# Weights of a two-layer decoder step stored in the order in which the kernel loads them

## The reference

```python
# mixers: dense projections in and out
proj = h @ w_in                              # mLSTM: (1024, 3088), NSA: (1024, 2608)
y = o @ w_out                                # (1024, 1024)

# NSA, compressed branch: blocks of 32 keys through a small MLP, first layer w1[c, 32, 64, 64]
first  = einsum('bnlcgd,cldh->bncgh', sub, w1[:, :16])
second = einsum('bnlcgd,cldh->bncgh', sub, w1[:, 16:])
ckv = einsum('bncgh,chd->bncgd', gelu(first[:, :-1] + second[:, 1:] + b1), w2)

# PEER, for each token
q = (x @ w_q).reshape(blk, 8, 256)           # w_q: (1024, 2048)
s1 = einsum('nhd,hkd->nhk', q[..., :128], sub_keys[:, 0])
s2 = einsum('nhd,hkd->nhk', q[..., 128:], sub_keys[:, 1])
# top 16 of each, top 16 of their 256 sums -> expert (8 heads x 16), gate = softmax
act = gelu(einsum('nd,nhkd->nhk', x, u_tab[expert]))
out = einsum('nhk,nhkd->nd', gate * act, v_tab[expert])
```

## Time and profile before

| | us |
|---|---|
| median of three runs | 2446.6 |
| the three runs | 2443.54, 2446.6, 2453.86 |
| the profiled execution | 2442.64 |
| its span, first to last instruction | 2440.4 |
| PE busy, DVE busy, POOL busy, ACT busy | 1919.6, 1482.9, 1445.5, 723.1 |
| moved by DMA | 805.62 MB, mean 330 GB/s |
| mean granted TensorE clock | 0.891 of full speed |

### The profile page before, as it was taken

The page is one execution under the profiler, slowest core; times in us unless marked ns, Lnnn a source line. Parts: engine busy times, 40 slices in busy tenths (PEclk is TensorE's granted clock), DMA queues, the critical chain, the costliest instruction groups (busy, mean ns, idle before and its releaser), DMA issues. The chain is left out here.

```text
span 2440.4 us, 22610 instructions
## 1 busy us (share of the span) xinstructions
PE 1919.6 (79%) x6982; PEld 949.8 (39%) x6982; DVE 1482.9 (61%) x3404; ACT 723.1 (30%) x1737; POOL 1445.5 (59%) x1285
## 2 busy tenths in 40 slices
PE   8997995999787776987879689875678777859666
PEld 6453682444343333545422255462123323313211
DVE  2234467885656544585884457759357776774753
ACT  2022122787556111421111125211123333312101
POOL 2111056668778775676677567744467666457674
PEclk9998997999898786898899879897899998979879
DMA  9053259999999999899999998998889999899897
GB/s 304 5 219 116 74 183 372 351 347 355 408 399 398 405 397 373 307 358 403 355 409 400 386 387 312 366 357 288 324 323 397 383 363 395 327 335 399 299 349 279
DMA packets 253950, 805.62 MB, mean 330 GB/s; under 512 B 41796, under 2 KB 46408, under 8 KB 244360
## 3 DMA queue, kind: packets, MB, share of 16 engines
q0 software_dynamic: 176496, 673.82, 72.5%
q1 hardware_dynamic: 77192, 130.37, 15.1%
q10 hardware_dynamic: 144, 0.00, 0.0%
HBM read 798.37 MB, written 14.04 MB: 333 GB/s over the span
## 5 line engine op out<-in xcount | busy, mean ns | idle before, releaser
L3259 PE MATMUL g_acc<-g_vrow,g_diag 128*128 128x512 f32 (+1 forms) x1524 | 812.0, 670 | 236.1 <-DMA g_vrow<-in_peer_v_dram,f_idx 131.3
L3113 POOL DMA_INDIRECT f_u<-in_peer_u_dram,f_idx x576 | 655.0, 1137 | 429.9 <-DVE g_dot L3200 170.3
L3129 POOL DMA_INDIRECT g_vrow<-in_peer_v_dram,f_idx x576 | 678.1, 1177 | 341.5 <-issue 145.6
L3200 DVE CUSTOM_DVE_ANT_0 f_u<-f_u,f_h 128x1024 f32<-128x1024 f32 x576 | 692.3, 1219 | 205.2 <-DMA f_u<-in_peer_u_dram,f_idx 160.2
L3259 PEld LDWEIGHTS g_acc<-g_vrow,g_diag 128*128 128x128 f32 (+1 forms) x1524 | 279.0, 197 | 686.5 <-issue 513.1
L3173 DVE SCALAR_TENSOR_TENSOR x<-g_vrow,g_w,x 128x1024 f32<-128x1024 f32 x195 | 249.7, 1281 | 93.1 <-DMA g_vrow<-in_peer_v_dram,f_idx 84.6
L3225 ACT ACTIVATE g_diag<-const,g_w 128x128 f32<-128x128 f32 (+1 forms) x381 | 132.0, 379 | 185.3 <-DVE g_w L3156 171.7
L1295 PE MATMUL g_side<-g_slab 128*128 128x512 f32 (+3 forms) x288 | 124.1, 570 | 46.5 <-DMA g_slab<-in_nsa_w_in_dram 45.9
L1155 PE MATMUL g_side<-g_slab 128*128 128x512 f32 x256 | 135.9, 614 | 4.2 <-ACT g_slab L1193 2.5
L2276 PE MATMUL g_side<-g_cmp_kT,g_q_blk 128*32 128x512 f32 x160 | 87.7, 632 | 41.6 <-DVE g_cmp_kT L2407 28.3
L1193 ACT ACTIVATE g_slab<-g_more 64x256 f32<-64x256 f32 x256 | 96.7, 378 | 63.5 <-PE g_more L1144 60.3
(11 more groups left out here) (418 smaller groups left out, 2427.2 us busy)
## 6 DMA issues: line engine op xcount, KB each, us to landing
g_slab<-in_nsa_w_in_dram SPq DMA_DIRECT2D x15, 2048.0 KB, 19.6
g_slab<-in_peer_w_q_dram SPq DMA_DIRECT2D x14, 2048.0 KB, 20.8
g_slab<-in_nsa_w_out_dram SPq DMA_DIRECT2D x6, 2048.0 KB, 21.3
f_u<-in_peer_u_dram,f_idx POOLq DMA_INDIRECT x576, 8.2
g_vrow<-in_peer_v_dram,f_idx POOLq DMA_INDIRECT x576, 8.0
g_slab<-in_state_win_kv_dram SPq DMA_DIRECT2D x8, 1024.0 KB, 8.6
out_win_s_dram<-in_state_win_kv_dram SPq DMA_DIRECT2D x1, 8128.0 KB
f_u<-in_mlstm_w_in_dram SPq DMA_DIRECT2D x2, 2048.0 KB, 17.2
```

The costliest lines, as they stand in the source:

```text
L3113: pool.indirect_dma_start(u[:, i % RU, :], None, u_table, bass.IndirectOffsetOnAxis(ap=idx[:, col:col + 1], axis=0), element_offset=layer ...
L3129: pool.indirect_dma_start(vrow[:, i % RV, :], None, v_table, bass.IndirectOffsetOnAxis(ap=idx[:, col:col + 1], axis=0), element_offset=lay ...
L3200: dve.tensor_tensor_reduce(row, row, h[:, t, :], 1.0, 0.0, ALU.mult, ALU.add, dot[:, g % 2, k:k + 1]).then_inc(dotted, 1)
L3259: mm = pe.matmul(acc[0:n, a, :], diag[:, q % (2 * GRP), 0:n], vrow[:, i % RV, a * 512:a * 512 + 512], start=first and on_pe[i] == on_pe[GR ...
```

## The change

The host lays out three kinds of weights anew before the launch; the kernel's loads follow.

- The five dense weights are stored as blocks of 512 columns, each [partition, chunk, column], so that a partition's 16 KB are one run. The columns left over (16 of the mLSTM input weight, 48 of the NSA input weight) are an array of their own, `<name>_rest`, in the same order.
- The sub-keys are stored as [d, head half, key]. SP loads them into `keys_T` itself. The transposes on PE, the copies on ACT and their semaphores go, in both routes; in the first route PE waits for `copied` 5 in their place, in the prompt's route the scores wait for `keys_in`.
- The compression's first layer is stored as [(position in pair, d), pair, half, h], and each of its two parts is one load with 4 KB per partition; the counts of the waits follow (7 loads become 5).

The same bytes are loaded, at the same points of SP's order. The core of the diff:

```diff
+def in_blocks(w):
+    layers, _, n = w.shape
+    full = n // WB * WB
+    w = w.reshape(layers, DC, P, n)
+    blocks = w[..., 0:full].reshape(layers, DC, P, n // WB, WB).transpose(0, 3, 2, 1, 4)
+    rest = w[..., full:].transpose(0, 2, 1, 3)
+    return blocks, rest
+
+def weight_block(I, name, layer, col, n):
+    if n == WB:
+        return I[name][layer, col // WB]
+    return I[name + "_rest"][layer]
...
 # front_stage, sync
-                    sp.dma_start(blocks[j][:], weight[:, :, col:col + n]).then_inc(w_in[j], 16)
+                    sp.dma_start(blocks[j][:], weight_block(I, "mlstm_w_in", 0, col, n)).then_inc(w_in[j], 16)
...
 # CachedBlocks.load_weights; the same in PromptWork.sync
         for c in range(2):
-            for f in range(2):
-                sp.dma_start(self.w1[:, c, :, f], I["nsa_cmp_w1"][0, c, f * CSTR:(f + 1) * CSTR].rearrange(
-                    "(k l) d h -> (l d) k h", l=2)).then_inc(self.weights_in, 16)
+            sp.dma_start(self.w1[:, c], I["nsa_cmp_w1"][0, c]).then_inc(self.weights_in, 16)
...
-    LOADS = 2 * 2 + 2 + 1
+    LOADS = 2 + 2 + 1
...
 # Projection.load; likewise w_out and w_q in PromptWork, RouteWork, DecodeWork, FirstRoute and the mLSTM stage
-        w_in = self.S.I["nsa_w_in"][0].rearrange("(c p) n -> p c n", p=P)
-        sp.dma_start(self.ring[t // 2][:, k % 2, :, 0:cols], w_in[:, :, col:col + cols]).then_inc(self.S.w_in[k % 2], 16)
+        sp.dma_start(self.ring[t // 2][:, k % 2, :, 0:cols], weight_block(self.S.I, "nsa_w_in", 0, col, cols)).then_inc(self.S.w_in[k % 2], 16)
...
 # PromptWork.sync, first tile
-            sp.dma_start(route.keys, I["peer_sub_keys"][1].rearrange("h s k d -> k (h s) d")).then_inc(route.keys_in, 16)
+            sp.dma_start(S.keys_T, I["peer_sub_keys"][1]).then_inc(route.keys_in, 16)
...
 # RouteWork.scores
-            pe.wait_ge(self.keys_copied, 2 * NJ)
+            pe.wait_ge(self.keys_in, 32)
...
 # FirstRoute.pe
         pe.wait_ge(self.keys_in, 16)
-        for k in range(NJ):
-            if k >= 2:
-                pe.wait_ge(self.keys_copied, k - 1)
-            self.turn_keys(pe, k)
-        pe.wait_ge(self.keys_copied, NJ)
+        pe.wait_ge(self.copied, 5)
...
 # FirstRoute.act; likewise in RouteWork.act
-        for k in range(NJ):
-            act.wait_ge(self.keys_turned, k + 1)
-            act.activation(S.keys_T[:, 4 * k:4 * k + 4, :], self.bank[k % 2].rearrange("p (c k) -> p c k", c=4), ACT.Copy
-                           ).then_inc(self.keys_copied, 1)
...
+def first_layer_of_blocks(w1):
+    layers = w1.shape[0]
+    w = w1.reshape(layers, 2, 2, CSTR // 2, 2, ADH, ADH)
+    return w.transpose(0, 1, 4, 5, 3, 2, 6).reshape(layers, 2, P, CSTR // 2, 2, ADH)
...
 # kernel(): laid_out = {**inputs, "const": CONST}
+    laid_out["peer_sub_keys"] = laid_out["peer_sub_keys"].transpose(0, 4, 1, 2, 3).reshape(-1, PK, HH, PK)
+    laid_out["nsa_cmp_w1"] = first_layer_of_blocks(laid_out["nsa_cmp_w1"])
+    for name in IN_BLOCKS:
+        laid_out[name], rest = in_blocks(laid_out[name])
```

More of the change, by code:

```diff
@@ L1859, in sync @@
         for c in range(2):
[L1860 to L1863, removed]
+            sp.dma_start(self.w1[:, c], I["nsa_cmp_w1"][0, c]).then_inc(self.cw_in, 16)
         for a in (1, 0):
@@ L1868, in sync @@
                 sp.wait_ge(self.multiplied, t + 1)
[L1869 removed]
+            sp.dma_start(proj.ring[0][:, a], weight_block(I, "nsa_w_out", 0, a * WB, WB)).then_inc(S.w_in[a], 16)
         sp.wait_ge(proj.saved, 16 * (3 * t + 3))
@@ L1999, in __init__ @@
         self.q_T = place(11264, [P, HH, P])
-        self.keys = place(15504, [P, HH, P])
         self.gain = place(13312, [P, D])
-        self.keys_in, self.keys_turned, self.keys_copied, self.q_stored, self.scored = (
-            st.sem("q_" + n) for n in ("keys_in", "keys_turned", "keys_copied", "stored", "scored"))
+        self.keys_in, self.q_stored, self.scored = (st.sem("q_" + n) for n in ("keys_in", "stored", "scored"))
     PROJ = 10
@@ L2036, in pe @@
             yield from at(p0 + b)
-            if t == 0 and b in (-2, 0, 2, 4):
-                self.turn_keys(pe, (b + 2) // 2)
             j, r = divmod(b, 6)
@@ L2082, in act @@
         p0 = beat + self.PROJ
-        if t == 0:
-            for k in range(NJ):
-                yield from at(p0 - 1 + 2 * k)
-                act.wait_ge(self.keys_turned, NJ + k + 1)
-                act.activation(S.keys_T[:, 4 * k:4 * k + 4, :], S.bank[k % 2].rearrange("p (c k) -> p c k", c=4),
-                               ACT.Copy).then_inc(self.keys_copied, 1)
         for j in range(NJ):
@@ L2691, with __init__ @@
 class FirstRoute:
-    def __init__(self, st, S, ranks, keys, u_ring, v_ring, more, acc, w_out_in, d_scores):
+    def __init__(self, st, S, ranks, keys_in, u_ring, v_ring, more, acc, w_out_in, d_scores):
         self.S, self.ranks, self.w_out_in = S, ranks, w_out_in
-        self.keys_in, self.keys_turned, self.keys_copied = keys
+        self.keys_in = keys_in
         place = S.slab.place
-        cmp_kT = S.cmp_kT[:].rearrange("p b a k -> p (b a k)")
         cmp_v = S.cmp_v[:].rearrange("p b g -> p (b g)")
@@ L2706, in __init__ @@
         self.q_TL = place(12800, [P, 4, P + NDEC])
-        self.keys = inside(cmp_kT, 0, [P, HH, P])
         self.gain = inside(cmp_v, 0, [P, D])
@@ L2739, in out @@
         mm.then_inc(self.summed, 1)
-    def turn_keys(self, pe, k):
-        for c in range(4):
-            mm = pe.transpose(self.bank[k % 2][:, c * P:(c + 1) * P], self.keys[:, 4 * k + c, :], self.S.M.ident)
-        mm.then_inc(self.keys_turned, 1)
     def project(self, pe, j):
@@ L3001, in __init__ @@
         self.route = RouteWork(st, S, self.proj, self.ranks)
-        keys = (self.route.keys_in, self.route.keys_turned, self.route.keys_copied)
-        self.first = FirstRoute(st, S, self.ranks, keys, u_ring, v_ring, more, acc, w_out_in, d_scores)
+        self.first = FirstRoute(st, S, self.ranks, self.route.keys_in, u_ring, v_ring, more, acc, w_out_in, d_scores)
         self.cached = CachedBlocks(st, S, self.first, [more[:, 0], more[:, 1]])
@@ L3356 @@
     arrays, I, O = {}, {}, {}
-    for name, value in {**inputs, "const": CONST}.items():
+    laid_out = {**inputs, "const": CONST}
+    laid_out["peer_sub_keys"] = laid_out["peer_sub_keys"].transpose(0, 4, 1, 2, 3).reshape(-1, PK, HH, PK)
+    laid_out["nsa_cmp_w1"] = first_layer_of_blocks(laid_out["nsa_cmp_w1"])
+    for name in IN_BLOCKS:
+        laid_out[name], rest = in_blocks(laid_out[name])
+        if rest.size:
+            laid_out[name + "_rest"] = rest
+    for name, value in laid_out.items():
         a = np.ascontiguousarray(value)
```

44 lines of the change are left out of this document (14 added, 30 removed).

## The result

The changed kernel takes 2385.7 us (median of four runs, 2371.9 to 2391.8) beside 2447.4 us for the kernel before: 61.7 us less, ratio 0.974 (95% interval 0.969 to 0.9785). The profiled execution of the changed kernel is the longest of its four, 2391.8 us (span 2389.6), 50.9 us less than the profiled one of before. 2386 was forecast. The total came out; several of the terms that make it up did not, and the rest of this text is about those.

The account below looks back on a forecast made before the run. No engine alone was taken as the bound: the DMA engines had 239 us of unfilled time in the interleaved stage, partly from late weight loads. Nine terms summed to 60.8 us (17 to 94), giving 2386 us, range 2353 to 2430.

Parts of the forecast that it names:

- A: First route, before the first gather: key transposes and copies removed, PE turns the normed tile sooner; gain 2.0 us (0 to 2.5).
- B: Cached blocks' start: the first layer comes some 35 us earlier, so DVE's late start goes; gain 11.3 us (2 to 21.6).
- C: First prompt tile: PE's waits for block 4 and first layer, mostly covered by DMA work; gain 4 us (1 to 5.5).
- G: Decode projection: PE short, two waits for blocks of 8.66 and 10.34 us go; gain 18 us (10 to 23).
- D: First prompt tile's route: PE's 7.45 us wait for a query block; gain 5 us (0 to 7.1).
- E: Second prompt tile: the same weight waits as in the first, as little room; gain 2 us (0 to 3.2).
- F: Second tile's route: PE's 8.46 us wait for query block 2 delays DVE's ranking; gain 8.5 us (4 to 13).
- H: Decode output: DVE's 6.53 us wait for joined parts, queued behind a 2 MB block; gain 5 us (0 to 8).
- I: Whole interleaved stage: cheaper transfers, 401 GB/s rising towards 409 during loads, over 37 blocks; gain 5 us (0 to 10).
- first rival: Dense blocks land no sooner; only keys and first layer gain, 17 us, total 2429 us; chance 0.13.
- second rival: Gather queue is the bound all along, engines freed earlier find no rows; gain 10 us, total 2437 us; chance 0.09.
- The third: Slower: 16 KB rows starve gathers during loads, 4.2 us per block where rings are empty; 2470 us at 20 blocks; chance 0.06.

Follow-up runs that it names:

- the first execution: First profiled execution of the changed kernel, no edit, against the one profiled execution of the kernel before: 2391.8 us, 50.9 us less.
- the three executions: Three profiled executions of the unedited changed kernel, each against the profiled execution of before: 50.9, 57.6 and 55.5 us gained.
- the first-layer experiment: Changed kernel with only the compression's first layer loaded as before, four loads of 256 KB with 256-byte runs: 2413.3 us, ratio 0.9847.
- the two repeats: The changed kernel measured twice more with no edit, beside other runs: 2387.7 us (ratio 0.9745) and 2381.5 us (ratio 0.9719).

## Why the prediction was right in sum, and where not

**Why the loads were late** was right in its core: time goes by rows, as many of one queue as of the other; that a turn is a single row, as the text had it, is not shown. The model's 15.4, 10.2 (for 4 KB) and 6.4 us stand beside 14.8, 9.9 to 10.0 and 6.1 to 8.0 us of rows. (The lower bound, 2.1 MB at 409 GB/s, is 5.1 us, not 5.2.) The landing of 8 us failed: 11.5. The step is "8 us with the latency by which the measured values exceed the model": it took 1.6 us from loads that stood in line behind one another, so that their time to the first row was already covered. With the queue empty most loads of the stage show about 3.5 us from SP's issue to its first row (1666.87 to 1670.31 in the kernel with a place for the gate columns) and 0.6 to 0.8 from the last row to PE. So "no wait above 3 us" failed as well: 6.88 us for block 4 in the first tile and 6.51 for the gate columns are left.

**The packets** fell by 53,600, not 59,000. Counted by size, blocks went from 46,080 rows to 5,760, the first layer from 12,288 to 768; but the gate columns stayed at 3,072 rows of 192 bytes, since their destination has gaps ("the gate columns 8 rows, 1.8 us" looked at the source alone), and the keys were only 1,024 rows of 2 KB before.

**A**, 2: the mechanism is right, PE turns the tile 0.15 us behind it instead of 2.0. To the first gather the keys are worth 3.0 us (1.8 in the first execution), over the upper end of 2.5: the term counted the wait and not the shorter turn. The rest of the 4.4, 2.7 and 4.7 us is the tile itself, ready to be normed at 246.09, 249.14 and 247.04 us in the three executions and at 248.75 before: scatter on both sides, which does not speak against "the front: nothing".

**B**, 11.3: 6.9, 14.6 and 16.7, all inside its bounds, and by the one profile of the first-layer experiment all of it the first layer's.

**C**, 4: 13.7 on average, far over its upper end of 5.5. The mechanism stands, the size failed: the room was read in a window of 10 us (955 to 965) and the text went no further. The stretch behind, and the decode projection for G, in the kernel before:

```profile
974.00:1019.40 45.40, 42.97 (x165) 25.32 (x164) 23.56 (x42) 15.46 (x44) 29.82 (x27) 0.83 0.87 312
1709.00:1791.60 82.60, 63.14 (x151) 18.03 (x151) 20.69 (x57) 11.63 (x27) 33.02 (x35) 0.88 0.80 285
```

From 974 to 1019.4, the slots behind the wait of 23.6 us, it had 45.4 x (1 - 312/409) = 10.8 us of room more. PE is short there before and after (busy 43.0 of 45.4 us, 41.8 of 45.8), so the slots can't catch up what the stall cost; the same slots after (943.2 to 989.0, shown above) run at 406 GB/s. Neither late load costs this alone: with the first layer as before the tile still gains 9.2 us, with blocks of 2 KB runs 10.9 to 12.6; the 13.7 are lost where the two follow each other.

**D**, 5: 3.7 to 6.9, right. **E**, 2: 4.5 on average against an upper end of 3.2, the same slip as in C, smaller.

**F**, 8.5: 5.3 on average, inside the bounds. "Here a stalled microsecond is a lost one" was too much: DVE's wait shrank by 2.4 us in the first execution and 5.4 in the third, since only 8.46 of its 19.97 us were PE's wait for the block, and DVE's ranking behind it runs as before (slots 384 to 396: 37.3 us in both).

**G**, 18: 9.8, under its lower end. The sum of the waits was right, but the step "8 us fits" failed: one wait went, in place of the other came one for the gate columns and block 4 behind them, 6.51 + 2.11 us. With those out of the way the stretch gives 19.7 us: the term was that of another kernel. The sign "near 70 us" came out, 70.3 us from slot 396 to 408, but the same slots took 82.6 before, not the 87 of the window in which the forecast was made.

**H**, 5: nothing that can be told from the scatter. DVE's wait shrank by 1.5 us alone. **I** shows in the rate, 408 to 410 instead of 401, but in no stretch of its own.

So a sum that came out within 1 us did so by luck, since two errors cancelled: first layer and keys were given 17 us (the first rival's working) and are worth 33.1 with the dense blocks in 2 KB runs (2448.2 - 2415.1); the dense blocks were given the other 44 and are worth 27.4. Alone, the first layer is worth 25.6 and the keys nothing that the time shows. 25.6 and 27.4 make 53.0 of the 60.5 us; the 7.5 left are close to what C lost only where both loads are late, 13.7 less 4.5 (the first layer late) less 1.1 to 2.8 (the blocks late), as far as the scatter lets one tell.

**The rivals.** The first, that dense blocks land no sooner, fell with 11.5 us: a 2 MB load over 128 partitions landed beside gathers after 19.4, 14.6 and 11.5 us with runs of 2, 4 and 16 KB, while the two queues together moved 401 to 423 GB/s in the three stretches counted above. The Trainium skill, "DMA: Bandwidth & Descriptors", "Rules for kernel authors", has 128 partitions and 1 MiB per DMA as enough for full bandwidth. The trace agrees with it on the rate; how soon a load lands is another matter, of which the rule does not speak.

The second rival, the gather queue as the bound all along, is nearly true of the blocks of the two prompt projections, whose stalls cost 1 to 6 us. One of its signs came half true elsewhere too. Waits for gathered rows and for query blocks before, then for gathered rows after:

```profile
DVE f_u L3200 <- DMA f_u<-in_peer_u_dram,f_idx: 160.2, 94, 6.3
...
PE g_acc L3259 <- DMA g_vrow<-in_peer_v_dram,f_idx: 131.3, 79, 11.6
...
PE g_side L2051 <- DMA g_slab<-in_peer_w_q_dram: 25.0, 5, 8.5
```

```profile
DVE f_u L3171 <- DMA f_u<-in_peer_u_dram,f_idx: 195.2, 108, 8.7
...
PE g_acc L3230 <- DMA g_vrow<-in_peer_v_dram,f_idx: 180.1, 100, 10.5
```

PE's waits for weights fell from 107.2 us (45.9 + 36.3 + 25.0) to 20.6, but its wait for V rows rose by 48.8 and DVE's for U rows by 35.0; the two repeats show the same (179.3 and 182.9, 197.2 and 192.6). So over half of what PE no longer waits for weights it now waits for gathered rows, and a wait that goes is not yet a gain. The rival's other sign, an unchanged rate of the stage, did not come: 370 GB/s instead of 362.

The third, that long rows starve the gathers, has its mechanism (gathers move 0.55 MB in a block's 6.2 us, a fifth of what the engines moved), but not its price: 16 KB is faster than 4 KB by 7.7 us and than 2 KB by 27.4.

## What to carry to other kernels

Where a plain load and an indirect gather share the DMA engines, count rows on both sides of the load, source and destination: for each of its rows one of the gather's passed here, so fewer and longer rows landed sooner at the same bytes. What a stall is worth is read from the room behind it until the rate is back at its peak (in the first prompt tile 3.2 and 10.8 us, beside 13.7 of gain; not tried on another stall), not from the stall and not from the next ten microseconds. And a wait that goes uncovers the next load in the queue: ask of each what it was issued on, before counting the gain.

## What the runs showed of the hardware that was not expected

- About 3.5 us pass from SP's issue to the first row of most loads beside a busy gather queue, with the load's own queue empty: as long as half the rows of a block of 16 KB runs (6.1 to 8.0 us). Two loads of the changed kernel that met no busy gather queue show 0.95 us: one at 124.92 us, before any gather, and one at 2098.85, where the engines moved 141 GB/s (2095 to 2100).
- A stall costs PE twice: behind 9.17 us of wait 6 matmuls took 4.91 us, behind 0.16 us 2.76 (the fences of the two kernels with packed gate columns). Over the 4.91 us after that wait the granted clock was 0.56, near the lower of its levels (1.2 and 2.4 GHz); over the 2.76 it was 1.00, the higher one, and PE had been busy 19.45 of the 19.6 us before. For the whole stretch it was 0.88 before, 0.93 after, and 1.00 with no stall in it.
